# Hybrid decoder layer on one core: convolution taps, sample states and decode chain placed anew in the attention loop

## The reference

```
u = rms_norm(x);  q,k,v,qi,ki,wi,bx,gb,gc,glu,zg,xbc,dt = split(u @ w_in)
A: 4 heads; an indexer scores the keys, each query keeps its best 128 (samples: 64) and attends over them
B: gb * conv3(gc * bx)
C: swish(layer_norm(conv31(ga * sigmoid(gg)) + cconv_b))
D: silu(conv4(xbc)), state-space scan in chunks of 128; samples: h = h*exp(dt*a) + dt*x*B, y = C.h
x += rms_norm(concat(A,B,C,D) @ w_out);   x += rms_norm((silu(h @ gate) * (h @ up)) @ down)
```

## Time and profile before

| | us |
|---|---|
| median of 3 runs | 1550.04 (1550.02 to 1550.23) |
| the profiled execution | 1550.77 |
| its span | 1549.2 |
| PE busy | 1427.5 (92%) |
| DVE busy | 794.0 (51%) |
| ACT busy | 550.9 (36%) |
| POOL busy | 200.9 (13%) |
| mean granted PE clock | 0.962 of 2.4 GHz |

### The profile page before, as it was taken

How to read it: one execution, slowest core, us unless ns; L and a number is a source line. 1 busy time by engine, 2 the same in 40 slices (tenths; PEclk the granted TensorE clock), 3 DMA queues, 4 the chain that set the end, 5 groups by cost and what they waited for, 6 DMA issues and landing times. The chain is left out here.

```text
span 1549.2 us, 29026 instructions
## 1 busy us (share of the span) xinstructions
PE 1427.5 (92%) x11720; PEld 1325.7 (86%) x11720; DVE 794.0 (51%) x1623; ACT 550.9 (36%) x907; POOL 200.9 (13%) x134
## 2 busy tenths in 40 slices
PE   4999888997999999999769999899989999999995
PEld 4888765896999999999657977768979999999994
DVE  5489866635444444222346897746264443442224
ACT  3444434534323233222344534264342232222222
POOL 1332233020000000000040422221200000000010
PEclk8999999998999999999879999899989999999997
DMA  6442242221333322233055323312313333323221
GB/s 224 130 133 69 69 108 59 97 85 47 93 93 95 91 85 83 76 93 93 8 202 141 99 69 82 96 58 86 96 55 96 88 88 95 95 63 92 88 70 56
DMA packets 222719, 141.21 MB, mean 91 GB/s; under 512 B 13514, under 2 KB 218674, under 8 KB 222102
## 3 DMA queue, kind: packets, MB, share of 16 engines
q1 hardware_dynamic: 220006, 132.55, 29.2%
q0 software_dynamic: 2624, 7.48, 1.6%
HBM read 124.64 MB, written 11.77 MB: 88 GB/s over the span
## 5 line engine op out<-in xcount | busy, mean ns | idle before, releaser
L1935 DVE TENSOR_TENSOR w_lo<-ring,w_hi 128x1024 fp32r<-128x1024 f32 (+2 forms) x164 | 179.3, 1093 | 399.3 <-ACT w_hi L1322 399.3
L620 PE MATMUL PS<-u_hi,w_hi 128*128 128x260 f32 x1600 | 325.9, 285 | 15.1 <-DVE u_lo L2056 11.4
L1322 ACT CAST w_hi<-ring 128x1024 fp32r<-128x1024 f32 (+2 forms) x168 | 158.9, 946 | 473.4 <-PE PS L620 473.4
L620 PE MATMUL PS<-u_hi,w_lo 128*128 128x260 f32 x1600 | 323.0, 283 | 0.0
L620 PE MATMUL PS<-u_lo,w_hi 128*128 128x260 f32 x1408 | 283.8, 283 | 0.0
L620 PEld LDWEIGHTS PS<-u_hi,w_hi 128*128 128x128 f32 x1600 | 247.1, 189 | 19.1 <-issue 13.5
L620 PEld LDWEIGHTS PS<-u_hi,w_lo 128*128 128x128 f32 x1600 | 248.0, 190 | 0.0
L620 PEld LDWEIGHTS PS<-u_lo,w_hi 128*128 128x128 f32 x1408 | 218.3, 189 | 0.0
L620 PE MATMUL PS<-hid_hi,w_hi 128*128 128x260 f32 x704 | 141.8, 283 | 3.5 <-ACTq L1479 3.5
L620 PE MATMUL PS<-hid_hi,w_lo 128*128 128x260 f32 x704 | 141.8, 283 | 0.0
L620 PE MATMUL PS<-hid_lo,w_hi 128*128 128x260 f32 x704 | 141.4, 282 | 0.0
(11 more groups left out here) (351 smaller groups left out, 2154.5 us busy)
## 6 DMA issues: line engine op xcount, KB each, us to landing
ring<-in_ffn_gate SPq DMA_DIRECT2D x44, 512.0 KB, 3.8
ring<-in_ffn_up SPq DMA_DIRECT2D x44, 512.0 KB, 3.8
ring<-in_w_in SPq DMA_DIRECT2D x36, 512.0 KB, 3.9
ring<-in_ffn_down SPq DMA_DIRECT2D x32, 384.0 KB, 3.4
ring<-in_ffn_down SPq DMA_DIRECT2D x32, 320.0 KB, 3.1
ring<-in_w_out SPq DMA_DIRECT2D x16, 512.0 KB, 4.4
x_store<-x SPq DMA_DIRECT2D x2, 2080.0 KB, 15.7
x<-x_store SPq DMA_DIRECT2D x2, 2080.0 KB, 7.8
```

Source lines behind the costliest of these rows:

```text
L620: ins = pe.matmul(to[:, h, :], w[:, k - base, :], a[k][:, h * HALF:(h + 1) * HALF], start=(begin and w is whi and a is a_hi), stop=(end an ...
L1322: act.copy(w_hi[part % 2][:, 0:n, :], raw[part % 4][:, 0:n, :]).then_inc(part_hi, 1)
L1935: dve.tensor_tensor(w_lo[part % 2][:, 0:n, :], raw[part % 4][:, 0:n, :], w_hi[part % 2][:, 0:n, :].bitcast(F32), ALU.subtract).then_inc(pa ...
```

## The change

It does eight things, all within the attention loop and the work just ahead of and behind it.
- Tap groups: instead of 4, 4 and 8 in steps 15, 16 and 17 there are 3, 3, 2, 2, 3 and 3 in steps 12 to 17. Both sums use bank 3; ACT copies the first out at the head of step 15, ahead of that step's exponential.
- Sample states: two in step 10, two in step 11, then one in each of steps 12 to 15, the last four through bank 2 alone. A state's first product is one instruction on both channel halves.
- Tap weights: made by DVE in step 10, not by POOL.
- Shifted copies: issued by SP ahead of its load of tile 15, not after that of tile 17.
- Decode chain: mask, turning, mix and pick on PE move from the ends of steps 3, 6, 8 and 9 to those of 2, 5, 7 and 8; on ACT and DVE its parts move by one step too. On DVE three top-k rounds come in step 0 and five in step 1 (four and four in steps 1 and 2 before), softplus moves from step 3 to 4, behind the decode probabilities. The state rows are turned within step 9, not at the head of step 10.
- DVE's convolutions move by a step: the samples' in 2, d0 to d3 in steps 5, 6, 8 and 9, d4 and d5 in 12 and 13, gates in 7 and 14.
- FEAT_SLABS: XBC are tiles 0 to 5, GG tiles 6 and 7.
- Ahead of the loop, 32 projection matmuls come before index_logits instead of 16 before and 16 behind.

```diff
- CS_BANK = [3, 2, 3, 2]
+ CS_BANK = [2, 3, 2, 3]
...
- FEAT_SLABS = [4, 6, 7, 8, 3, 2, 0, 5, 1]
+ FEAT_SLABS = [6, 7, 8, 4, 3, 2, 0, 5, 1]
...
- STATES_FROM = 11
+ STATES_AT = {10: (0, 1), 11: (2, 3), 12: (4,), 13: (5,), 14: (6,), 15: (7,)}
  FIRST_FFN = [(q, [k]) for k in range(5) for q in range(3)] + [(0, [5, 6, 7]), (2, [5, 6, 7]), (1, [5, 6, 7])]
- TAP_SETS = {15: 4, 16: 4, 17: 8}
+ TAP_SETS = {12: 3, 13: 3, 14: 2, 15: 2, 16: 3, 17: 3}
...
+     if f == 15:
+         sp.wait_ge(gate_in, 2)
+         sp.wait_ge(tap_edges, 8)
+         for b in range(8):
+             for j in range(4):
+                 sp.dma_start(shifted[b][32 * j:32 * j + 32, j:SEQ],
+                              feat[32 * (b % 4):32 * (b % 4) + 32, GA + b // 4, 0:SEQ - j])\
+                     .then_inc(taps_in[b // 4], 16)
      sp.dma_start(raw[(f + 2) % 4], cols("w_in", FEAT0 + s * W + c * P, P)).then_inc(tile_in[(f + 2) % 4], 16)
- sp.wait_ge(gate_in, 2)
- sp.wait_ge(tap_edges, 8)
- for b in range(8):
-     for j in range(4):
-         sp.dma_start(shifted[b][32 * j:32 * j + 32, j:SEQ],
-                      feat[32 * (b % 4):32 * (b % 4) + 32, GA + b // 4, 0:SEQ - j]).then_inc(taps_in[b // 4], 16)
...
- feature_products(PER_PART)
+ feature_products(2 * PER_PART)
  index_logits()
  key_products(0)
- feature_products(PER_PART)
  key_products(1)
...
- def spread_states(i):
-     if i == 0:
+ def state_bank(b):
+     return bank(2 + b % 2 if b < 4 else 2)
+ def spread_states(b):
+     if b == 0:
          pe.wait_ge(picks_ready, 1)
-     pe.wait_ge(decd_dve, i + 1)
-     for b in (2 * i, 2 * i + 1):
-         pick = ident_r[0:NS, b:b + 1].broadcast_to([NS, P])
-         pe.matmul(bank(2 + b % 2), pick, bc_hi[:, :], start=True, stop=False)
-         pe.matmul(bank(2 + b % 2), pick, bc_lo[:, :], start=False, stop=True).then_inc(decd_pe, 1)
+     pe.wait_ge(decd_dve, 1 + b - (b % 2 if b < 4 else 0))
+     pick = ident_r[0:NS, b:b + 1].broadcast_to([NS, P])
+     pe.matmul(state_bank(b), pick, bc_hi[:, :], start=True, stop=False)
+     pe.matmul(state_bank(b), pick, bc_lo[:, :], start=False, stop=True).then_inc(decd_pe, 1)
...
- pe.wait_ge(decd_dve, NS // 2 + 1)
+ pe.wait_ge(decd_dve, NS + 1)
...
-         pe.wait_ge(decd_dve, NS // 2 + 1)
+         pe.wait_ge(decd_dve, 5)
      else:
-         pe.wait_ge(tails_ready, 4)
+         pe.wait_ge(conv_c_done, 1)
  for b in range(4):
-     last = pe.matmul(bank(3 - c)[32 * b:32 * b + 32, 4 * g:SEQ], tap_w[:, c, b, TAP_GROUPS - 1 - g, :],
+     last = pe.matmul(bank(3)[32 * b:32 * b + 32, 4 * g:SEQ], tap_w[:, c, b, TAP_GROUPS - 1 - g, :],
...
- if j == 10:
-     turn_state_rows()
  if j == 16:
      turn_tails()
  if j == -1:
      two_logits(0)
  feature_products(step_products(j))
- if STATES_FROM <= j < STATES_FROM + NS // 2:
-     spread_states(j - STATES_FROM)
+ for b in STATES_AT.get(j, ()):
+     spread_states(b)
...
+ if j == 9:
+     turn_state_rows()
  feature_products(step_products(j))
- if j == 3:
+ if j == 2:
      decode_mask()
- if j == 6:
+ if j == 5:
      decode_prob_turn()
+ if j == 7:
+     decode_mix()
  if j == 8:
-     decode_mix()
- if j == 9:
      decode_pick()
...
- pe.wait_ge(decd_dve, NS // 2 + 1)
+ pe.wait_ge(decd_dve, NS + 1)
+ pe.wait_ge(tails_ready, 4)
...
- pe.wait_ge(conv_c_done, 1)
...
- act.activation(feat[:, GG + c, 0:SEQ], bank(3 - c), ACT.Identity, bias=pcol("cconv_b", c))\
+ act.activation(feat[:, GG + c, 0:SEQ], bank(3), ACT.Identity, bias=pcol("cconv_b", c))\
...
- if j == 5:
+ if j == 4:
      decode_exp()
- if j == 9:
+ if j == 8:
      act.wait_ge(dec_pe, 4)
      act.copy(sample_mix, bank(2)).then_inc(mix_kept, 1)
+ if j == 9:
+     decode_out()
  if j == 10:
-     decode_out()
- if j == 11:
      act.wait_ge(decd_dve, 1)
      act.activation(edt[:, 0], edt[:, 0], ACT.Exp).then_inc(dt_exp, 1)
+ if j == 15:
+     conv_c_out(0)
  if j < len(STEPS):
      blk, h = STEPS[j]
      keys = (blk + 1) * P
...
- if j == 10:
-     act.wait_ge(decd_pe, 1)
-     act.copy(bc_hi[:, :], bank(2)[0:NS, :]).then_inc(bc_hi_ready, 1)
...
+ if j == 9:
+     act.wait_ge(decd_pe, 1)
+     act.copy(bc_hi[:, :], bank(2)[0:NS, :]).then_inc(bc_hi_ready, 1)
...
- if j == 6:
+ if j == 4:
      conv_d_samples_out()
...
- conv_c_out(0)
  conv_c_out(1)
...
- def sample_states(i):
-     if i == 0:
+ def sample_states(b):
+     if b == 0:
          dve.wait_ge(dt_exp, 3)
-     if i % 2 == 0:
-         dve.wait_ge(ssm_half[i // 2], layer * 16 + 16)
-     settle()
-     dve.wait_ge(decd_pe, 2 * i + 3)
-     two = [(q, 2 * i + q, bank(2 + q), c) for q in range(2) for c in range(2)]
-     for q, b, bc, c in two:
-         step(dve.tensor_scalar(prod_n[:, q, c, :], bc[:, c * P:(c + 1) * P], dtx[:, c, b:b + 1], None, ALU.mult))
-     settle()
-     for q, b, bc, c in two:
+     if b % 4 == 0:
+         dve.wait_ge(ssm_half[b // 4], layer * 16 + 16)
+     settle()
+     dve.wait_ge(decd_pe, b + 2)
+     bc = bank(2 + b % 2 if b < 4 else 2)
+     prod = prod_n[:, b % 2]
+     step(dve.tensor_tensor(prod, bc[:, 0:W].rearrange("p (c n) -> p c n", c=2),
+                            dtx[:, :, b:b + 1].broadcast_to([P, 2, P]), ALU.mult))
+     settle()
+     for c in range(2):
          h = ssm[:, 2 * b + c, :]
-         step(dve.scalar_tensor_tensor(h, h, edt[:, 0, c, b:b + 1], prod_n[:, q, c, :], ALU.mult, ALU.add))
-     settle()
-     for q, b, bc, c in two:
-         step(dve.tensor_tensor_reduce(prod_n[:, q, c, :], ssm[:, 2 * b + c, :], bc[:, W + c * P:W + (c + 1) * P],
-                                       1.0, 0.0, ALU.mult, ALU.add, y_dec[:, c, b:b + 1]))
-     settle()
-     dve.sem_inc(decd_dve, 1)
-     if i == NS // 2 - 1:
+         step(dve.scalar_tensor_tensor(h, h, edt[:, 0, c, b:b + 1], prod[:, c, :], ALU.mult, ALU.add))
+     settle()
+     for c in range(2):
+         last = dve.tensor_tensor_reduce(prod[:, c, :], ssm[:, 2 * b + c, :], bc[:, W + c * P:W + (c + 1) * P],
+                                         1.0, 0.0, ALU.mult, ALU.add, y_dec[:, c, b:b + 1])
+         if c == 0:
+             step(last)
+     last.then_inc(decd_dve, 1)
+     if b == NS - 1:
+         dve.wait_ge(decd_dve, NS + 1)
          dve.sem_inc(ssm_done, 1)
+ def tap_weights():
+     dve.wait_ge(tap_cols_ready, 17)
+     dve.wait_ge(dec_pe, 5)
+     n = 2 * 4 * TAP_GROUPS
+     dve.tensor_tensor(tap_w.rearrange("p c b g m -> p (c b g) m"),
+                       const("tap_mask").unsqueeze(1).broadcast_to([P, n, 32]),
+                       tap_col.rearrange("p c b g -> p (c b g)").unsqueeze(2).broadcast_to([P, n, 32]),
+                       ALU.mult).then_inc(tap_w_ready, 1)
...
          self_scores()
+         dve.wait_ge(dec_dve, 1)
+         decode_best(3)
      elif j == 1:
-         dve.wait_ge(dec_dve, 1)
-         decode_best(TOPK_SAMPLE // 16)
+         decode_best(5)
+         decode_mask()
      elif j == 2:
-         decode_best(TOPK_SAMPLE // 16)
-         decode_mask()
+         conv_d_samples()
      elif j == 3:
+         decode_logits()
+     elif j == 4:
+         decode_probs()
          softplus()
-     elif j == 4:
-         decode_logits()
      elif j == 5:
-         decode_probs()
-         conv_d_samples()
+         conv_d(0)
      elif j == 6:
-         conv_d(0)
-     elif j == 7:
          decode_columns()
          conv_d(1)
+     elif j == 7:
+         gate_c()
      elif j == 8:
-         gate_c()
+         conv_d(2)
      elif j == 9:
-         conv_d(2)
+         conv_d(3)
+         state_rows()
      elif j == 10:
-         state_rows()
-         conv_d(3)
-     if j == 15:
-         conv_b(0)
-     if STATES_FROM <= j < STATES_FROM + NS // 2:
-         sample_states(j - STATES_FROM)
-     if j == 11:
+         tap_weights()
+     for b in STATES_AT.get(j, ()):
+         sample_states(b)
+     if j == 12:
          conv_d(4)
-     elif j == 12:
+     elif j == 13:
          conv_d(5)
          settle()
          dve.sem_inc(conv_d_done, 1)
-     elif j == 13:
+     elif j == 14:
          gate_b()
+     elif j == 15:
+         conv_b(0)
  conv_b(1)
...
- def tap_weights():
-     pool.wait_ge(tap_cols_ready, 17)
-     pool.wait_ge(dec_pe, 5)
...
- if f == 15:
-     tap_weights()
```

More of the change, by code:

```diff
@@ L2140, in shifted_edges @@
                             pool.memset(t[:, 0:4], 0.0).then_inc(tap_edges, 1)
-                    def tap_weights():
-                        pool.wait_ge(tap_cols_ready, 17)
-                        pool.wait_ge(dec_pe, 5)
-                        n = 2 * 4 * TAP_GROUPS
-                        pool.tensor_tensor(tap_w.rearrange("p c b g m -> p (c b g) m"),
-                                           const("tap_mask").unsqueeze(1).broadcast_to([P, n, 32]),
-                                           tap_col.rearrange("p c b g -> p (c b g)").unsqueeze(2).broadcast_to([P, n, 32]),
-                                           ALU.mult).then_inc(tap_w_ready, 1)
                     for f in range(2, len(feat_tiles)):
```

## The result

The changed kernel takes 1563.43 us (median of 4 runs, 1562.75 to 1564.31) against 1550.13 us of the kernel before (4 runs, 1550.02 to 1551.73): ratio 1.0086, 95% interval 1.0070 to 1.0102. It is 13 us slower; the forecast was 1564. The profiled execution took 1563.87 us with a span of 1562.2, 13.0 above the span of before.

A forecast was written before the change was run, and what follows sets the result against it. PE bounds the kernel, busy 1427.5 of 1549.2 us. Profiled 1550.77 plus 3.7 for the loops plus 10.2 of clock gives 1564.7, the median 0.73 below: 1564 us, range over the cases 1549 to 1573.

The forecast's parts named there:

- idle sum: PE's waits in the first layer's attention loop, ten terms from step 1 to the tails: 20.3 us.
- (a): Step 1: three top-k rounds now come first, the first scaling ends at 155.0, and PE waits 1.7 us.
- (b): Tile 6, first sigmoid tile: eviction queued behind five rounds, mask and exponential, plus a table load; PE waits 4.0 us.
- (c): End of step 3, tile 7, sigmoid again: eviction with table load loses its cover; 3.0 us in place of 0.68.
- (d): Decode exponentials, probabilities and softplus come late: PE waits 1.1 us for scaling, then 2.1 us for tile 8's eviction.
- (e): Evictions ending steps 6 and 9 lose decode matmuls beside them, 1.85 us each; step 8's stays near 1.4.
- The late half: From step 10: DVE waits (6.3 us) and clock loss (2.85) go; 2.0 at step 14, 1.25 new before tails.
- Floor: PE's own work in the first layer's loop at full clock: 111.5 less 2.85, 108.7 us.
- Clock: Half-clock stretches behind PE's long waits in the attention loop: 5.1 us a layer, 10.2 in all.
- Rival 1: DVE and ACT keep up in steps 1 to 5, gaining 4.3 us a layer: 1541 us, chance 0.17.
- Rival 2: PE's clock holds through the loop's short waits, so only 3.7 us remain: 1554 us, chance 0.2.
- Rivals 3 and 4: DVE bounds steps 10 and 11: 1571 us, chance 0.13; tap sets wait for shifted copies: 1570 us, chance 0.03.

The follow-up runs named there:

- second experiment: Late half of the change alone on the kernel before, with decode chain and shifted copies where they were: 1552.23 us, ratio 1.0004.
- the last kernel: Changed kernel with sigmoid tiles back as tiles 0 and 1 and top-k rounds four and four in steps 1 and 2: 1544.52 us, ratio 0.9952.

## Why the prediction was right

It named the direction, the kinds of wait, most of their places and the size. That 1564 lies 0.6 us from the measured median is luck: the loops grew by 20.9 us where 13.9 was predicted, and 7.9 us won outside them, of which the prediction had only a hint, made up for it. Its idle sum, too, is right by terms that were off on both sides. By its steps, first layer:

- **Idle sum, 20.3 predicted, 20.4 measured.** (a) and (b) together 5.7 predicted, 5.70 + 2.99 = 8.7 measured. The first scaling was to end at 155.0 and ended at 157.2; PE was to arrive at 153.4 and came at 151.6. Of the 4.0 that (a) is too long, the 1.8 by which PE came early is no loss, for it is no longer waited ahead of the loop. The other 2.1 is the step that failed: the reordered work "can only bring it to the same wait sooner", but it also brought POOL's tile 1.9 us earlier (151.00, not 152.88), onto the small product. The run with POOL held back took just this out. (b) alone was 2.99, not 4.0: PE was late, so ACT was free for it, and what is left is the bare eviction with its load.
- **(c)** 3.0 predicted, 3.10.
- **(d)** 3.2 predicted, 0.54 measured. PE reached tile 8's end at 188.5, not 184.1, held up in (a) and at half clock from 180 to 182.6; ACT and DVE were nearly through by then. The softplus run shows that its place was worth nothing. Nor did the wait of step 5 for scaled probabilities come, one of the signs named.
- **(e)** 1.85, 1.4, 1.85 and 2.0 predicted; 1.69, 1.47, 1.69 and 1.86 measured; ahead of the tails 1.25 and 1.30 (the profile names no releaser there, but ACT's eviction with its load ends at 273.56 and PE starts at 273.66).
- **The late half.** No wait for DVE after step 1, and none for the eviction at the end of step 12; tap weights 2.28 us (2.2 predicted); the shifted copies were issued by 222.7 (219 predicted) and nobody waited. What the prediction didn't say is that this half gains nothing if done alone (second experiment).
- **Floor.** The same 919 to 920 instructions take 111.0 us at clock 1.00 in the last kernel, so the floor was 111.0 and not 108.7. Taking half of the slow stretch behind the 5.04 was nearly right: the same work takes 5.82 us there (239.17 to 244.99) and 3.20 in the last kernel (239.39 to 242.59), so 2.6 and not 2.85. The 128 tap products, now in runs of two and three groups, take 21.8 us in place of 20.9. The other 1.2 no row assigns.
- **Clock.** Against that floor the clock cost 116.06 - 111.04 = 5.0 us in layer one and 7.5 in layer two; 5.1 each was predicted. The size was near, the places were not: PE was slow behind (a), behind (c) and behind the wait of 1.86 in step 14 (0.50 from 158 to 162 and from 180 to 182.6, 0.57 from 258 to 262), and at 1.00 behind (b), from 166 to 174. Nor was the stretch behind (a) "hidden by the wait in (b)": ACT stood idle for 1.48 us until PE ended tile 6, and in the run with PE kept busy that tile was taken up 1.43 us earlier.

Rival 1 (faster, 1541) was wrong on this kernel, and right on where it is decided: with the sigmoid tiles and the rounds put back, the early half costs less and the time is 1544.5. Rival 2 fell, since the clock didn't hold (0.95 and 0.93). What spoke for it, "seven waits up to 1.7 without a fall", held in the first layer only: in the second layer of the kernel before, the clock was 0.77 from 970 to 974 behind a wait of 1.55, and 0.65 from 988 to 992 behind one of 1.29. Rivals 3 and 4 fell: no wait of PE in steps 10 to 12 and none for the copies.

On tables, each activation starts 1.29 us after its load begins (165.69 to 166.98, 177.48 to 178.77), and the load at 179.39 begins as the activation before it ends. The 1380 ns of drain that the Trainium skill counts (ScalarE: Activation LUTs, What ACT_TABLE_LOAD costs) show in no row here; the measurement decides for 1.28 a switch.

## What to carry to other kernels

Moving a chain a step earlier is paid where it lands: price the steps that take it, and try the late half and the early half apart before judging the change as a whole; here the change less two of its own moves takes 1.3% less than the change (0.9952/1.0086). When an instruction moves, list what each other engine has beside it afterwards, short instructions too. Try the smallest piece alone as well: one moved instruction, the tap weights, gave 0.9970, and no larger set of moves beat it beyond its interval. Undoing edits one at a time may understate them: two that each left a wait above 3 us gave 0.0134 together and 0.0106 by their sum, with a better clock in the traces, though the times leave the difference open.

## What the runs showed of the hardware

A DVE instruction on two SBUF tensors doesn't slow in proportion to its size when POOL works: 8x8 elements took 2.29 us in place of 0.16, starting 0.08 us after POOL's instruction and ending 0.02 after it, in both layers. It goes the other way too; POOL's tile that started inside DVE's tap weights (221.63 to 223.91) took 3.79 us, not 2.35:

```profile
222.37 3.79 POOL L2127 TENSOR_TENSOR w_lo<-ring,w_hi 128x1024 fp32r<-128x1024 f32 x1 [7.70 <-ACT w_hi L1200]
```

The Trainium skill (SBUF — State Buffer, SBUF: two separate sides) describes this as a lock on a shared pair of ports: whichever instruction starts first keeps it to its end, and the other blocks. These rows agree.

A slow stretch can move instead of going away. With PE kept busy through the wait of step 1, 158 to 162 ran at 1.00 in place of 0.50, and 166 to 170, behind the next wait, at 0.58 in place of 1.00. With step 1's wait at 2.8 (rounds) and at 1.8 (old product order) it stood there too, at 0.50.

For waits near 2 us the rows give no rule. Behind one of 1.86 the clock fell in the changed kernel (258 to 262, 0.57) and held in the last one (1.00 from 249 to 257). Behind one of 1.94 it held in that kernel's first layer and fell in its second (0.82 from 940 to 944, 0.75 from 944 to 948).
